# One 1 MB weight block held on chip, and ten row buffers in place of twelve, in a one-core decoder layer

## The reference, cut to what matters

```python
proj = h @ w_in                                   # 1024 tokens x 1024
a    = pool_mixer(...)                            # trailing-window means, per-group linear map
m    = ssm_mixer(...)                             # conv, chunked scan, gate, norm, projection
h    = layer_norm(ALPHA * h + (sigmoid(gp) * a + sigmoid(gs) * m) @ w_out)
q    = (h @ w_q)                                  # 8 heads, 256 columns each
# product-key top-16 of 128 x 128 experts per head: 8 * 16 = 128 experts a token
hk   = einsum('td,thkd->thk', h, expert_u[idx])   # one gathered 4 KB row per token and expert
act  = gelu(hk) * gate
h    = layer_norm(ALPHA * h + einsum('thk,thkd->td', act, expert_v[idx]))
```

## Time and profile before

| what | value |
|---|---|
| median of 3 runs | 3649.55 us |
| profiled execution, its time | 3651.32 us |
| its span | 3649.6 us |
| traffic | 1389.71 MB, 381 GB/s over the span |
| PE / DVE / POOL / ACT busy | 79% / 73% / 57% / 29% |

### The profile page before, as it was taken

One profiled execution on the slowest core, in us unless ns is written; L12 is line 12 of the kernel. 1 busy time (PEld: TensorE's weight loads), 2 busy tenths in 40 slices (PEclk: granted clock), 3 DMA queues, 4 the chain that ended last, 5 costly groups with the idle time before them and its releaser, 6 DMA issues.

```text
span 3649.6 us, 46261 instructions
## 1 busy us (share of the span) xinstructions
PE 2878.3 (79%) x16076; PEld 2053.1 (56%) x16076; DVE 2678.8 (73%) x5760; ACT 1066.4 (29%) x2756; POOL 2069.4 (57%) x1839
## 2 busy tenths in 40 slices
PE   8986989789889879999988779999977853443443
PEld 7886887677777427777775437787754410000000
DVE  3418756899975888777776887777776886668667
ACT  5522632244322214444313114444212110001000
POOL 0003433576655667766666676667766676555552
PEclk9998999899899879999999879999988866555555
DMA  6557999999999999999999999999999999999997
GB/s 247 204 229 305 379 373 384 367 376 398 380 343 360 410 409 398 400 409 402 400 410 411 410 399 385 407 403 393 410 383 411 402 400 415 421 421 422 421 421 312
DMA packets 315415, 1389.71 MB, mean 381 GB/s; under 512 B 35504, under 2 KB 41008, under 8 KB 250672
## 3 DMA queue, kind: packets, MB, share of 16 engines
q0 software_dynamic: 262656, 1073.86, 73.9%
q1 hardware_dynamic: 51232, 308.18, 21.3%
q10 hardware_dynamic: 1296, 4.72, 0.3%
HBM read 1382.43 MB, written 4.19 MB: 380 GB/s over the span
## 4 chain that ended last, share of the span: by engine, by line
DMA 25%; PE 25%; POOL 12%; issue 5%; DVE 4%; ACT 1%; DVEq 0%; POOLq 0%; ACTq 0%
POOL rowbuf L607 10%; PE main L650 10%; DMA rowbuf<-ev,idx 8%; DMA rowbuf<-euv,idx 5%; PE vbank L738 4%; DMA ring<-euv,idx 3%; PE main L658 3%; PE main L869 2%; PE main L854 2%; DMA merged<-euv,idx 2%; DVE acc L1738 2%; DMA xT<-euv,idx 2%; PE turn L721 2%; DMA rowbuf<-eu,idx 1%; DMA late<-euv,idx 1%
## 5 line engine op out<-in xcount | busy, mean ns | idle before, releaser
L607 POOL DMA_INDIRECT rowbuf<-eu,idx x722 | 847.2, 1173 | 801.3 <-DVE hdot L1712 280.4
L607 POOL DMA_INDIRECT rowbuf<-ev,idx x717 | 774.5, 1080 | 397.7 <-issue 191.8
L1712 DVE CUSTOM_DVE_ANT_0 rowbuf<-rowbuf,hb 128x1024 f32<-128x1024 f32 x637 | 778.8, 1224 | 162.9 <-DMA rowbuf<-eu,idx 96.0
L650 PE MATMUL main<-xT,ring 128*128 128x256 f32 (+1 forms) x4480 | 804.7, 340 | 13.5 <-DMA ring<-wblocks 10.8
L650 PEld LDWEIGHTS main<-xT,ring 128*128 128x128 f32 x4480 | 720.2, 193 | 99.0 <-issue 29.7
L738 PE MATMUL vbank<-rowbuf,vdiag 64*64 64x512 f32 x2992 | 494.4, 758 | 260.9 <-DMA rowbuf<-ev,idx 138.9
L1738 DVE SCALAR_TENSOR_TENSOR acc<-rowbuf,hact,acc 128x1024 f32<-128x1024 f32 x427 | 549.8, 1288 | 89.6 <-DMA rowbuf<-ev,idx 80.3
L738 PEld LDWEIGHTS vbank<-rowbuf,vdiag 64*64 64x64 f32 x2992 | 104.2, 156 | 572.4 <-ACT vdiag L1090 318.2
L1090 ACT ACTIVATE vdiag<-spots,hact 128x64 f32<-128x64 f32 x531 | 167.9, 344 | 549.3 <-DVE hact L1721 343.9
L854 PE MATMUL main<-late,ring 128*128 128x256 f32 (+1 forms) x1280 | 237.0, 349 | 32.2 <-issue 21.2
L854 PEld LDWEIGHTS main<-late,ring 128*128 128x128 f32 x1280 | 211.2, 199 | 57.3 <-issue 25.1
(11 more groups left out here) (251 smaller groups left out, 3845.3 us busy)
## 6 DMA issues: line engine op xcount, KB each, us to landing
ring<-wblocks SPq DMA_DIRECT2D x280, 1024.0 KB, 8.1
rowbuf<-eu,idx POOLq DMA_INDIRECT x722, 12.8
rowbuf<-ev,idx POOLq DMA_INDIRECT x717, 12.6
pw<-poolw SPq DMA_DIRECT2D x20, 256.0 KB, 9.5
h_out<-acc ACTq DMA_DIRECT2D x8, 512.0 KB
xT<-xt SPq DMA_DIRECT2D x3, 1024.0 KB, 13.4
zy<-x SPq DMA_DIRECT2D x3, 1024.0 KB, 13.7
rowbuf<-euv,idx POOLq DMA_INDIRECT x84, 20.0
```

Source lines behind the costliest of these rows:

```text
L607: pool.indirect_dma_start(rows[r], None, (eu, ev)[table], bass.IndirectOffsetOnAxis(ap=idx[c % 2][:, u, k:k + 1], axis=0)).then_inc(row_re ...
L650: last = pe.matmul(dst_[:, ct * tc:(ct + 1) * tc], w[:, k, ct * P:(ct + 1) * P], src[:, k, 0:tc], start=(k == 0), stop=(k == KD - 1))
L1712: last = dve.tensor_tensor_reduce(r, r, h, 1.0, 0.0, ALU.mult, ALU.add, hdot[:, g % 2, k:k + 1])
```

## The change

A tile of 1 MB, `kept` (128 partitions x 8 KB), is added. Block 55 goes there instead of `ring[3]`, is loaded in chunk 0 only, and in chunks 1 to 4 SP only raises `w_ready[3]` in its place. The room comes from the row buffers: `ROWS` is 10 instead of 12. In the tail `kept` is one more double buffer beside the ring, and `rowbuf` gives five instead of six, so there are 16 as before; `WIDE`, the number of double buffers that are filled before those of `rowbuf`, is 11 instead of 10.

```diff
-ROWS = 12
+ROWS = 10
+KEPT = BLOCKS - 1
...
-WIDE = 10
+WIDE = 11
...
         ring = [sb(f"ring{r}", [P, KD, 256]) for r in range(RING)]
+        kept = sb("kept", [P, KD, 256])
...
-        both = [ring[r][:, :, :].rearrange("p k n -> p (k n)") for r in range(RING)]
+        both = [b[:, :, :].rearrange("p k n -> p (k n)") for b in ring + [kept]]
...
                     sp.wait_ge(block_done, c * BLOCKS + b + r + 1)
-                    sp.dma_start(ring[r][:, :, :], wblocks[ds(b + r, 1), :, :].rearrange("o p (k n) -> (o p) k n", k=KD)
+                    if b + r == KEPT and c:
+                        sp.sem_inc(w_ready[r], 16)
+                        continue
+                    sp.dma_start((kept if b + r == KEPT else ring[r])[:, :, :], wblocks[ds(b + r, 1), :, :].rearrange("o p (k n) -> (o p) k n", k=KD)
                                  ).then_inc(w_ready[r], 16)
...
-                if n == RING + 4:
+                if n == RING + 5:
...
-                return ring[n % RING]
+                return kept if turns * RING + n == KEPT else ring[n % RING]
```

## The result

The changed kernel takes 3692.28 us (median of 5 runs, 3683.83 to 3694.82) against 3649.55 (3647.32 to 3651.78): ratio 1.0107, 95% interval 1.0095 to 1.0118, so 39 us slower by the ratio and 43 by the medians. The forecast was 3670 in a range of 3641 to 3700. The profiled execution took 3689.2 us, its span is 3687.2.

The account below looks back on a forecast made before the run. No single engine bounds the body; PE and transfers are both nearly full in A of chunks 3 and 4, transfers alone in D. 3651.3 + 28.4 - 7.7 = 3672.0, less 1.8 to the median: 3670 us, range 3641 to 3700.

Parts of the forecast that it names:

- Saved loads: D parts of chunks 1 to 4: four loads fewer, valued at three of four, 7.7 us saved, at most 10.3.
- Two buffers fewer make the kernel slower: Body: POOL blocks two issues earlier at shallow-queue stalls, 28.4 us slower, bounds 0 and 51 us.
- Ten x 2.84: Ten POOL stalls ending with PE, seven in scan parts of chunks 3 and 4, each 2.84 us later: 28.4 us.
- The signs: A parts, chunks 3 and 4: PE share about 94%, POOL stalls about 2.8 us longer, PE's row wait 3 to 4 us.
- That PE holds the row: At the stall ending at 1664.36, POOL waits for a buffer whose row, twelve places earlier, PE held.
- While the queue is deep two rows fewer in it cost nothing: Where rows take 17 to 18 us to land, transfers stay full and rows merely queue less long: no cost.
- Chunk 2: VectorE is busiest, most rows should land well ahead: no cost; five places counted only in the upper bound.
- The tail: Still 16 double buffers, `kept` as the eleventh; transfers at 421 GB/s throughout, so as long as before.
- Ten are plenty: Rival: ten buffers keep the engines full, only the saving counts, 3639 to 3642 us; chance of faster 0.13.
- about cancel: Rival: only four stalls move the end, 11.4 us against 7.7 to 10.3 saved, 3651 to 3653 us; chance 0.15.
- Much slower: Rival: ten rows tie PE and VectorE, a second round trip per `j` in chunks 3 and 4, above 3700; chance 0.07.
- The rule on bubbles and missing buffers: Repeating equal gaps on the engine that should be full mean too few buffers; kernel already short, two fewer go wrong.

Follow-up runs that it names:

- e1: Kernel before with twelve row buffers and no kept tile, block 55 simply not loaded in chunks 1 to 4: 3642.62 us against 3650.03.
- e2: Kernel before with ten of its twelve row buffers used in the body, all four loads kept: 3707.38 us, ratio 1.0152.
- e7: Kernel before, twelve buffers, PE sums no rows in the A parts of chunks 3 and 4, VectorE does them all: 3678.78 us, ratio 1.0077.
- e8: Kernel before with no PE rows in the A parts of chunks 3 and 4 and ten buffers in the body: 3729.55 us, ratio 1.0215.
- e11: Kernel before, twelve buffers, with the odd blocks' weight loads left out in chunks 1 to 4: 3576.82 us, ratio 0.9791.
- e12: Kernel before with the odd blocks' weight loads left out in chunks 1 to 4 and ten buffers in the body: 3608.23 us, ratio 0.9873.
- e10: Kernel before, twelve buffers, the guest in the scan's scratch tile lent from part C on instead of W: 3652.46 us against 3653.68.
- e3: Kernel before with eleven of its twelve row buffers used in the body, nothing else changed: 3672.69 us, ratio 1.0064.

## Why the prediction was right or wrong

**Saved loads: right.** 7.7 us was the value, 7.3 is measured (e1), though the factor of three in four had no row behind it and the interval is 3 to 12 us. In e1 they show in the D parts, as said; in the changed kernel chunk 4's D part is not shorter (+0.7). The 276 loads named for the ring were 275, the 276th being the one into `kept`.

**Two buffers fewer make the kernel slower: right in direction, half in size.** 28.4 us was the term, 55 is measured in the body alone (e2), some 46 in the changed kernel (39 + 7). The time came out inside the range because its upper end allowed 18 places, not because the places were counted well.

**"Ten x 2.84", the A parts of chunks 3 and 4: right in size by luck.** Seven places, 19.9 us, were to be PE's waiting; the parts grew by 17.5 us in the changed kernel, 18.2 in e2. But PE's idle time grew by 7.7 us only (3.4 and 4.3; 7.0 in e2), a third of the term, and at the one place looked at again the shift was 1.4 us. The remaining 10 us or so are PE's busy time, which the prediction took as fixed: it had no term for the granted clock, which fell after PE's longer waits. The signs say the same. PE's busy share did not go down to 94%, it is 96% in chunk 3 and 95% in chunk 4 (97% and 96% between the same marks before), POOL's stalls did not all grow by 2.8 us, and PE waited 2.26 us at this place, not 3 to 4.

**That PE holds the row: not needed.** Without PE rows in these parts the price stays (e7, e8), in a kernel that is bound otherwise. What survives is that the price in A comes with full transfer engines: with a tenth of chunk 3 A's traffic taken away (362 GB/s for 404) the two A parts lose 4.3 us instead of 18.2 (e11, e12). Which swing of the consumers empties the stock when PE holds no row was not looked at in a run of its own.

**"While the queue is deep two rows fewer in it cost nothing": the step that failed.** It was judged by the rate, and the rate did stay: chunk 3's C part runs at 408 GB/s with twelve and with ten. Yet it takes 103 us for 98, and at the same rate that is 2.0 MB more that came within it: 1.4 MB of rows (2.7 rows) and 0.6 MB of weights, counted in the traces by queue. Fewer rows had been requested ahead: 784 for 786 when VectorE begins C, 841 for 844 when it begins W. In the chain this part holds two row transfers before, three after:

```profile
1847.89 19.45 DMA rowbuf<-ev,idx
...
1868.99 18.61 DMA rowbuf<-ev,idx
...
1889.26 16.18 DMA rowbuf<-ev,idx
```

Then the W part loses 3 us more at 365 GB/s for 406. I had three places in C, W and the start of D of chunks 3 and 4, 8.5 us; C and W of these chunks lost 16.8 us in the changed kernel, and 24.3 with chunk 2. They lose nearly as much with half of the weights (21.7 in e12 against e11, 24.6 in e2), so the full engines alone do not make it dear there. What does, is open: with two buffers fewer they lose, with one more in C (e10) they gain nothing. A kernel that takes the rows off PE in W alone would tell whether its holding them matters there; it was not tried.

**Chunk 2: too low.** Its A part was to cost nothing, because VectorE is the busiest there and rows should land well ahead; it lost 9.2 us. The five places there stood only in the upper bound. Part of W's loss came back in D (-9.1, of which 4.5 are the saving's by e1): there the transfers bound, and what W did not fetch or compute D caught up.

**The tail: right**, -0.5 us.

**The rivals.** "Ten are plenty" and "about cancel" are out by e2 and e3. "Much slower" is out by the A parts, which grew by 15.1 and 2.4 us where it asked for some 8 us in each of eight `j`; its own sum, 63 us on top of the 3670, is also well above the 3700 that bounds it. On the page "DMA: Bandwidth & Descriptors" of the Trainium skill, section "Anatomy of one DMA — SWDGE (gpsimd) path", the estimate for a single row was 3.2 us and the sum by it 3640; it is a fit for one transfer, and here rows compete: 5.87 us after the stall, 16 to 19 in the C part. The rule on bubbles and missing buffers (page "Perfetto Trace Analysis", section "Optimization Strategy") is borne out, by five buffer counts from 8 to 13, although the visible gaps grew at only three of the seven places in A when two buffers went.

## What to carry to other kernels

When on-chip room is moved from prefetch buffers to a resident operand, price both in the same coin: here the resident megabyte saved 7 us for four loads, and the same megabyte as two gather buffers was worth some 50. Such a buffer works all through the kernel, the load is saved four times. A stall's visible length did not tell the price of a buffer; where two resources are each nearly full, change the number of buffers by one in both directions and measure. A transfer queue that stays full was no proof that a buffer less is free: two to three rows fewer had been requested when the next part began. And compare the same piece of the program before and after, with PE's idle time, busy time and granted clock side by side: most of what the longer waits cost chunk 3's A part appeared as busy time.

## What had not been expected of the hardware

Halving the weight traffic left the A part of chunk 3 at its old length (405.9 us for 405.4) although the transfer engines had shown a share of 1.01 there; a share near 1 was not a sign that fewer bytes would be faster there. It fell to 0.94 without any gain, with PE busy 97% of the part. C and W of the same chunk, at 1.02 and 1.03 with PE busy 85% and 87%, became 17.7 us shorter.

PE's waits for rows cost more than their length. In chunk 3's A part the granted clock went to its lower level for 10.2 us at a wait of 4.27 us and for 6.8 us behind one of 2.26 us, where in the kernel before, with waits of 1.56 us at most, it stayed at the upper one.
